# The inverse of a chunk's triangle from 32x32 products on four places of the array, and full-array products gathered in runs

## What is computed

```
def step(s, inp):
    w_t, k_t, v_t, kk_t, kka_t = inp[:5]
    sa = jnp.einsum('bhvk,bhk->bhv', s, kk_t)
    s = (s * w_t[:, :, None, :] - sa[..., None] * kka_t[:, :, None, :]
         + v_t[..., None] * k_t[:, :, None, :])
    y = jnp.einsum('bhvk,bhk->bhv', s, inp[5]) if len(inp) == 6 else None
    return s, y

s_fin, ys = lax.scan(step, s0, xs, reverse=reverse)
```

## Time and profile before

| what | us |
|---|---|
| median of 3 runs | 2094.38 |
| profiled execution | 2096.83 |
| its span | 2095.0 |
| one iteration of `mixing` (vt of j to vt of j + 1) | 109.13 |
| of it, from vt to the handover | 70.16 |
| of it, from the handover to the next vt | 38.97 |
| last iteration, from vt to the scan | 48.72 |
| `experts` | about 1003 |

### The profile page before, as it was taken

The page is one execution under the profiler, slowest core; times in us unless marked ns, Lnnn a source line. Parts: engine busy times, 40 slices in busy tenths (PEclk is TensorE's granted clock), DMA queues, the critical chain, the costliest instruction groups (busy, mean ns, idle before and its releaser), DMA issues. The chain is left out here.

```text
span 2095.0 us, 46331 instructions
## 1 busy us (share of the span) xinstructions
PE 1978.0 (94%) x20126; PEld 1160.5 (55%) x20126; DVE 607.6 (29%) x1299; ACT 485.1 (23%) x861; POOL 104.1 (5%) x136
## 2 busy tenths in 40 slices
PE   3589999999999999999859999999999999999997
PEld 1158787777778777778344344434444344434442
DVE  2135444535363535453241111111111111111111
ACT  1123333332423242434111111111111111111111
POOL 0001111101020202020000000000000000000000
PEclk9689999999999999999959999999999999999998
DMA  6922111111110202020238999999999999999995
GB/s 254 375 64 66 42 36 43 46 33 56 33 56 23 66 13 76 13 72 3 94 158 324 422 422 422 422 422 422 422 422 422 422 421 422 422 422 422 422 422 233
DMA packets 75328, 489.70 MB, mean 234 GB/s; under 512 B 9616, under 2 KB 10688, under 8 KB 21168
## 3 DMA queue, kind: packets, MB, share of 16 engines
q1 hardware_dynamic: 75056, 487.43, 57.9%
q0 software_dynamic: 128, 0.11, 0.0%
HBM read 486.46 MB, written 1.05 MB: 233 GB/s over the span
## 5 line engine op out<-in xcount | busy, mean ns | idle before, releaser
L1368 PE MATMUL PS<-raw,hgT 128*64 128x512 f32 x2120 | 471.8, 598 | 0.0
L1368 PEld LDWEIGHTS PS<-raw,hgT 128*64 128x64 f32 x2120 | 147.5, 137 | 298.0 <-issue 297.7
L1414 PE MATMUL PS<-raw,actT 128*64 128x512 f32 x1056 | 232.2, 592 | 0.0
L701 PEld LDWEIGHTS PS<-raw 64*64 64x64 f32 x6144 | 191.8, 135 | 45.2 <-issue 45.2
L701 PE MATMUL PS<-raw 64*64 64x64 f32 x6144 | 213.2, 220 | 0.0
L670 PE MATMUL PS<-arena 128*128 128x256 f32 x640 | 166.5, 399 | 10.6 <-ACT arena L514 10.6
L636 PE MATMUL PS<-arena 128*128 128x256 f32 x512 | 170.6, 424 | 0.0
L1414 PEld LDWEIGHTS PS<-raw,actT 128*64 128x64 f32 x1056 | 75.9, 137 | 150.7 <-issue 150.7
L1353 PEld LDWEIGHTS PS<-take,MT 128*128 128x128 f32 x1088 | 127.3, 196 | 31.3 <-issue 26.8
L1483 DVE TENSOR_SCALAR back<-cst,now 128x128 f32<-128x128 f32 x66 | 19.9, 343 | 428.4 <-PE PS L1419 428.4
L1353 PE MATMUL PS<-take,MT 128*128 128x64 f32 x1088 | 132.0, 281 | 4.4 <-DVE take L1464 4.4
(11 more groups left out here) (297 smaller groups left out, 2019.6 us busy)
## 6 DMA issues: line engine op xcount, KB each, us to landing
raw<-in_w_exp SPq DMA_DIRECT2D x397, 1024.0 KB, 16.4
arena<-in_w_blk SPq DMA_DIRECT2D x67, 512.0 KB, 3.6
raw<-in_w_ada SPq DMA_DIRECT2D x24, 1024.0 KB, 17.9
arena<-in_w_out SPq DMA_DIRECT2D x8, 512.0 KB, 3.5
arena<-in_lora_up SPq DMA_DIRECT2D x8, 192.0 KB, 3.9
cst<-in_consts SPq DMA_DIRECT2D x1, 1330.5 KB, 5.9
arena<-in_ctx SPq DMA_DIRECT2D x2, 512.0 KB, 7.6
xl<-in_x SPq DMA_DIRECT2D x2, 512.0 KB, 8.9
```

Source lines behind the costliest of these rows:

```text
L701: ins = mm(out[H[h], c, :], lhsT[H[h], c, :], rhs[H[h], c, :], start=True, stop=True)
L1368: ins = mm(PS[H[h], GU + g, :], hgT[:, s, :], raw[:, s, cols], start=False, stop=s == KT - 1, skip_group_check=True)
L1414: ins = mm(PS[H[m], Y, :], aT[:, q, H[h]], raw[:, KT + q, cols], start=q == 0 and h == 0, stop=q == 3 and h == 1, skip_group_check=True)
```

## The change

- The masked blocks on the diagonal are kept compact: `NF`, `NP`, the powers and `YB` are 8 chunks of 32 columns (128x256 instead of 128x512). `unit32` multiplies them: for each chunk four products of 32x32x32 on the four diagonal 32x32 places, 32 products for a direction instead of 16.
- G1 and G2 make only the blocks that are used, with 64 rows and 32 columns of the array each: 32 products for a direction, and in G1 16 more for the block off the diagonal (`EB`).
- TP, ET and Y64 become 16 products of 32x32x32 each for a direction.
- `YB` is spread into the 64x64 `YY` by two DVE operations, and Y64 is added to the block off the diagonal.
- The 32 `ahead` products stand in five runs of 8, 8, 4, 6 and 6.
- `loras(j + 1)` now comes before `receptance(j + 1)`; the waits are exchanged, since U0 lies in banks "c" now.
- BT is turned in bank "b" right behind AT, KT behind Y16.
- On ACT, `spread` is cut in `square_dev` and `deviation`, behind vt and behind BT. On DVE, `norms(j + 1)` and the reciprocal of `merge` stand behind Y16, the bonus product behind Y64.
- The other four operations of `merge` go to POOL, as five (the addition of `ln_b` joins them).

```
-                    unit("G1", "c", d, BE[d], AL[d])
-                    ahead(j + 1, d)
+                    out = bk32("c", d)
+                    blocks(out, BE[d], AL[d])
+                    for c in range(NC):
+                        for h in (0, 1):
+                            ins = mm(out[G[2 * h + d], NC + c, :], BE[d][H[h], c, B[d]], AL[d][H[h], c, B[1 - d]],
+                                     start=True, stop=True)
+                    ins.then_inc(S["G1_mm"], 1)
+                run(0, 8)
...
+                for job, b, lhsT, rhs, need in (
+                    ("N2P", "c", NF, NP, ("G4_ev",)),
+                    ("N2F", "a", NP, NF, ("AT_ev",)),
+                    ("Y2", "b", Q0P, YB, ("N2P_ev", "y1_dn", "BT_ev")),
+                    ("N4P", "c", Q0F, Q0P, ("N2F_ev",)),
+                    ("N4F", "a", Q0P, Q0F, ()),
+                    ("Y4", "b", Q1P, YB, ("N4P_ev", "Y2_ev")),
+                    ("N8P", "c", Q1F, Q1P, ("N4F_ev",)),
+                    ("N8F", "a", Q1P, Q1F, ()),
+                    ("Y8", "b", Q0P, YB, ("N8P_ev", "Y4_ev")),
+                    ("N16P", "c", Q0F, Q0P, ("N8F_ev",)),
+                    ("Y16", "a", Q1P, YB, ("N16P_ev", "Y8_ev")),
+                ):
                     for d in (0, 1):
                         waits(d, *need)
+                        unit32(job, b, d, lhsT, rhs)
+                run(16, 20)
+                if j < KT - 1:
+                    squares(j + 1)
...
+                def unit32(job, b, d, lhsT, rhs):
+                    out = bk32(b, d)
+                    for c in range(NC):
+                        for g in range(4):
+                            ins = mm(out[G[g], c, :], lhsT[d][G[g], c, :], rhs[d][G[g], c, :], start=True, stop=True)
+                    ins.then_inc(S[f"{job}_mm"], 1)
...
                 if j < KT - 1:
+                    loras(j + 1)
                     receptance(j + 1)
-                    loras(j + 1)
...
+            def merge(j):
+                pool.wait_ge(S["rstd_dn"], j + 1)
+                step(tt(yc, yc, yq, ALU.mult))
+                step(ts(yc, yc, c_(j, "ln_w"), c_(j, "ln_b"), ALU.mult, ALU.add))
+                step(tt(yc, yc, bo, ALU.add))
+                step(tt(yc, yc, gy_two[j % 2], ALU.mult))
+                step(tt(MT[:, j, :], yc, cv_two[j % 2], ALU.add), S["mt_dn"])
```

More of the change, by code:

```diff
@@ L576, in _ @@
                 if j:
[L577 to L584, removed]
+                    square_dev(j - 1)
+                for job, out, b in (("AT", AT, "a"), ("BT", BT, "b")):
                     for d in (0, 1):
@@ L586, in _ @@
                         halves(job, out[d], d, bank[b][d])
[L587 to L592, removed]
-                        mix("k", k_sh, K_BANK, T, j + 1)
-                    if job == "N16P" and j < KT - 1:
-                        square(j + 1)
-                    if job == "X" and j < KT - 1:
-                        norm(j + 1)
-                    for d in (0, 1):
-                        copy(job, out, d, b)
@@ new lines, in _ @@
+                for job, out, b in (("N8P", Q0P, "c"), ("N8F", Q0F, "a")):
+                    for d in (0, 1):
+                        copy32(job, out, d, b)
+                if j < KT - 1:
+                    square(j + 1)
+                for d in (0, 1):
+                    copy32("N16P", Q1P, d, "c")
+                if j < KT - 1:
+                    norm(j + 1)
+                for d in (0, 1):
+                    copy32("TP", TP, d, "c")
+                for d in (0, 1):
+                    copy("X", X, d, "a")
@@ L689, in _, with run @@
             for j in range(KT):
+                def run(start, end):
+                    for n in range(start, end):
+                        ahead(j + 1, n)
                 def waits(d, *products):
@@ L773, in _ @@
[L773 to L791 removed]
+                    turn("BT", bank["b"][d], BE[d])
@@ new lines, in _ @@
+                for d in (0, 1):
+                    unit("X", "a", d, KF[d], VT)
+                for d in (0, 1):
+                    waits(d, "TP_ev")
+                    out = bk32("c", d)
+                    for c in range(NC):
+                        for h in (0, 1):
+                            g = 2 * h + d
+                            ins = mm(out[G[2 * h + 1 - d], c, :], EB[d][G[g], c, :], TP[d][G[g], c, :], start=True, stop=True)
+                    ins.then_inc(S["ET_mm"], 1)
@@ new lines, in _ @@
+                run(20, 26)
+                for d in (0, 1):
+                    waits(d, "ET_ev", "X_ev")
+                    out = bk32("a", d)
+                    for c in range(NC):
+                        for h in (0, 1):
+                            g = 2 * h + 1 - d
+                            ins = mm(out[G[2 * h + d], c, :], ET[d][G[g], c, :], YB[d][G[g], c, :], start=True, stop=True)
+                    ins.then_inc(S["Y64_mm"], 1)
+                run(26, 32)
+                for d in (0, 1):
+                    waits(d, "Y64_ev", "KT_ev")
+                    unit("WT", "b", d, AT[d], YY[d])
@@ L806, in out_rows @@
+                for d in (0, 1):
+                    unit("U0", "c", d, YY[d], X[d])
                 def out_rows(n):
```

191 lines of the change are left out of this document (95 added, 96 removed).

## The result

The changed kernel takes 2186.95 us, the median of 4 runs (2182.93 to 2193.08), beside 2095.30 us for the kernel before in the same runs: 1.0439 times as long, with an interval of 1.0412 to 1.0467. The prediction said 1949 us and a range up to 2066.

A forecast was written before the change was run, and what follows sets the result against it. TensorE's own list was taken as the bound. Seven iterations at -19.7 us (-138), the last -9 and the tail +1.6 took 2096.83 to 1951.4, or 1949 us at the median; range 1930 to 2066.

The forecast's parts named there:

- Part 1, the runs: Full-array blocks between small-product units: 35 become 6, saving 29 x 0.34 = 9.9 us in each of seven iterations.
- Part 2, the small products: Inverse on TensorE: 32 units (29.9 us) become 34 groups at 0.53 us (18.0), 11.9 us less an iteration.
- u: Cost of one group of small products on TensorE, as long as the busiest place needs for 8; taken as 0.53 us.
- if packets follow each other without a gap, 60 products in 1.03 us: TensorE's instruction supply: at 1.03 us a packet, 17 ns a product and 0.55 us a group.
- the slow ones: Rival, chance 0.19: instruction packets requested one after another, pause 0.3 to 0.8 us, group 0.7 to 0.96, total 1995 to 2066.
- the front end: Rival, chance 0.13: TensorE's front end limits small products, a group costing beyond 1.08 us, 1.87 at 58 ns a product.
- The clock: Rival, chance 0.07: TensorE's clock falls because the new products fill only a quarter of the array.
- Part 3: Waits that appear in each iteration: 0.8 us before Y16 and 1.3 us at the handover.
- The handover: End of iteration: the new order delays receptance copy and table load before `fill`, 1.3 us more idle.
- The wait of 0.8 us before Y16: Doubling: TensorE waits for ACT's square and copies behind DVE's keys operations, 0.7 to 0.9 us, taken as 0.8.
- Part 4, the last iteration: Iteration without runs or handover: cheaper products, but uncovered ACT copies; -9 us, between -12 and -6.
- Part 5, the tail: Last tile's `merge`: POOL's operations take 3.85 us against DVE's 1.87, one operation (0.39) goes; +1.6 us.

The follow-up runs named there:

- `bench`: Kernel before plus a TensorE-only stage of small products, written out and in loops; 512 of 32x32 took 28.35 us written out, 13.97 us from a loop.
- `fill_dummy`: Changed kernel plus two dummy full-array 128x256 products ahead of each direction of each doubling step; 2213.97 us, 1.0561 times the kernel before.
- `bench2`: Kernel before plus a stage of longer loops and of 32-product groups with 1, 2 or 3 full-array products; groups took 1.71, 1.88 and 2.17 us.

## Why the prediction was wrong, point by point

- **Part 1, the runs: right.** 0.34 us a block; -8.4 measured alone for 27 blocks.
- **Part 2, the small products: the step that failed.** The price of a group where its instructions are present is right: u = 0.53 forecast, 0.54 measured. No row of before shows the 0.53, which was the author's estimate; the line through the paces for 64 and 256 columns makes 16 records of 32 columns 0.51 us, and the runs showed 31.3 ns a record on one place, and four places side by side at 8.9. What failed is the sentence "if packets follow each other without a gap, 60 products in 1.03 us". 1.03 us is how long a packet is under way, read from its share of the queue's time; I took a latency for a rate. In the doubling a packet takes the same (1.9% of 16 engines over 35.59 us are 1.08 us for each of ten), but bursts start 3.60 us apart in the mean, so 32 products cost 1.8 us in a row of nothing else, and with what lay ready u = 35.59 / 22 = 1.62. Of the two rivals that named instructions, the slow ones (0.7 to 0.96) had the mechanism and too small a pause, and the front end (1.08 to 1.87) had the size. Doubling: +23 to +26 us an iteration over the 12.5 forecast with its wait of 0.8.
- **The sentence "before, TensorE never waited for a packet" was true and said too little.** Before, 64 unbroken 64x64 products take 3.73 us of array, and packets come every 3.35 to 4.0. The kernel stood at the limit, and nothing in its profile shows how near.
- **The clock: a consequence.** It was a rival by itself, on the ground that small products fill a quarter of the array. The loops of small products on four places ran 14 and 11 us at 1.00 from start to end. Where the same products came in bursts with holes it fell (0.59 over the 28.35 us of `bench`, 0.60 and 0.55 in the doublings). It costs little inside the doubling, since a burst at half clock (1.93 us) is still over before the next packet, but it holds on behind it: the run of four took 3.42 us at 0.61 in place of 1.99 at 1.00. In the iteration from 517.76 us what isn't doubling takes 119.24 - 38.06 = 81.2 us, where I forecast 89.4 - 12.5 = 76.9 and `fill_dummy`, with the clock up, has 121.35 - 42.28 - 1.06 = 78.0. So of the 29.8 us by which this iteration missed the forecast some 3 are the clock's by this comparison, about 1 the supply's in the Gram products, and 25.6 the doubling's.
- **Part 3.** The handover was right (+1.3 an iteration, 9.5 in all). The wait of 0.8 us before Y16 is nowhere in the trace: TensorE was the later of the two.
- **Part 4, the last iteration:** 34 us over the forecast with the scan and the tail, by the same cause and at a low clock. The first window below is from vt to behind the first burst of the doubling (219 records from 1011.15 on), the second from there to TP. Of the 5 us of waits for ACT that I expected, 1.8 show: 0.8 before the first product of YB, 1.0 before WT.

```profile
994.59:1014.80 20.21, 16.45 (x695) 14.76 (x694) 8.18 (x18) 7.57 (x20) 4.15 (x7) 0.83 0.02 4
1014.80:1052.73 37.93, 19.98 (x1198) 18.26 (x1197) 4.57 (x10) 6.61 (x18) 0.00 (x0) 0.52 0.02 5
```

- **Part 5, the tail: right.** From the end of the reciprocal on DVE (1113.81) to POOL's last operation (1117.75) it is 3.94 us, 3.85 forecast:

```profile
1112.06 1.75 DVE L1037 RECIPROCAL raw<-raw 128x256 f32<-128x256 f32 x1 [0.15 <-ACT raw L599]
```

```profile
1117.03 0.72 POOL L479 TENSOR_TENSOR MT<-raw 128x256 f32<-128x256 f32 x1
```

- **The chances.** The front end beyond u = 1.08 had 0.13, and the range left it out on its far side. Its lower rival stopped at a pause of 0.8 us for no reason in the rows; the bound should have been the nearest row that speaks of a rate. That is the last window of the earlier trace rows, 31.20 us of units without an `ahead`, in which the queue brought eight packets, one in 3.9 us (the line below). The fastest row that the prediction had, units at 0.93 us, makes it 3.7 us a packet. By these two u is 1.87 to 1.95.

```profile
q8 instruction: 8, 0.13, 1.6%
```

Left open: what a packet's 3.35 to 4.0 us consist of beside the 1.03 to 1.08 of its transfer, since no row shows when it is asked for. That only one is on its way at a time is argued from the spacing and not shown. Open, too, is whether the doubling in a loop would hold. Its first nine jobs are three equal rounds, and one round is three packets, which by `bench2` would stay with TensorE, but its waits would hang on values that change from turn to turn, and it wasn't tried.

## What to carry to other kernels

Before cutting TensorE's products smaller, count instructions, not only array time: here 256 instructions, or 64 float32 products of whatever size, took 3.35 to 4.0 us wherever the array was faster, unless they came from a loop of no more than four packets. A product that lasts less is then paid at about 55 ns, unless large products stand in the same packet. So large products belong in runs while the others are slower than the supply, and between the small ones when these are faster. And the time that one transfer takes isn't the rate at which they come: a resource's rate is bounded by the fastest row in which it was really asked for it.

## What was unexpected of the hardware

- TensorE's instructions came one packet ahead only (two at the very end of the running one), every 3.35 to 4.0 us in the bursts of the changed kernel and of `bench`, although a loop of four packets is kept and runs from its second turn at 9.7 ns a matmul record.
- Four places together start a record every 8.9 ns, each place one every 36. One place by itself starts one every 31.3, two together one every 17.3.
- A turn of a loop of 32 products cost TensorE about 0.3 us beside them (0.87 us a turn in `bench`, of which 64 records at 8.9 ns are 0.57).
- On one place, with no hole at all, the clock fell from 1.00 (1178 to 1183 us of `bench`) to 0.50 (1187 to 1199) in the course of 23.5 us. On four places such products kept it at 1.00 over 13.97 us. In the loop of four packets it had fallen in the first turn (0.69 over those 11 us) and rose again in the turns without holes, while nothing but 32x32 products ran:

```profile
1104.50:1113.90 9.40, 9.17 (x1070) 8.95 (x1060) 0.00 (x0) 0.00 (x0) 0.00 (x0) 1.00 0.00 0
```
